# The front of a second transformer block, reordered: raw rows transposed, norms behind the matmuls, pool projection before the softmax transposes, a split router

## The chip, the core and the metric

One core of a Trainium2 chip runs the whole program in one launch. The metric is device time in microseconds (us) from start to end; lower is better. The engines named below are TensorE (PE; PEld is its weight load), VectorE (DVE), ScalarE (ACT), GpSimd (POOL) and SyncE (SP, which issues the weight loads). Each runs its own list of instructions in order and waits on semaphores.

## The reference, cut to what matters

Two blocks run one after the other on x of 256 tokens by 1024, all in float32. The first ends in a gated convolution FFN and a final RMS norm; its output is the second block's x:

```python
return rms_norm(h, norm_final_g)                  # end of the first block
# second block
h = rmsnorm(x, g_attn_norm)
u, q_lat, kv_lat, k_r = split(h @ w_in)           # 512, 256, 128, 32 columns
y_pool = pool_mixer(u, w_pool, b_pool, pool_scale)   # (window means - u) @ w_pool + b_pool, times pool_scale
y_attn = mla_attention(q_lat, kv_lat, k_r, ...)   # 8 heads: 64 plain + 32 rotated columns, causal softmax
mix = concat(rmsnorm(y_pool, g_out_pool), rmsnorm(y_attn, g_out_attn))
x = x + mix @ w_out
h = rmsnorm(x, g_ffn_norm)
x = x + moe(h, w_router, b_router, w_gate_up, ...)   # top 4 of 32 experts
return rmsnorm(x, g_final)
```

## The kernel before

The 256 tokens are two blocks of 128 rows (b = 0, 1); the 1024 columns are eight tiles of 128. `t.h` holds the residual rows, tokens on partitions. A matmul over the columns needs the rows transposed, which TensorE does against an identity, four 128x128 tiles into one bank of PSUM (eight banks), after which DVE or ACT copies the bank to SBUF.

Two lists written by hand, `RESULTS` and `RESULTS2`, fix the order in which the banks are filled and who drains each. A bank is opened when the result eight places earlier has been drained (`open_bank`); `filled` and `drained` turn a name into a semaphore and its value. For the second block the order is: `nT` (transposed normed rows), `lat0`, `lat1` (latents of q and kv and the raw rope columns), `u0`, `u1`, `qlT`, `kvT` (latents transposed), `qq`, `kv` (projections, drained by ACT), `qT`, `kT` (heads transposed), `s0` to `s7` (scores), `pm0`, `pm1` (pool matmul), `pss` (sums of squares of the pool output), `pt0` to `pt7` (softmax transposed), `av` (attention times values), `yt` (its transpose), `pa` and `pp` in turn (attention's and pool's half of the output projection, 512 columns for each of two row blocks), `rT` (rows transposed for the router), `lg` (logits), `rk` (ranks within an expert).

Norms: DVE and ACT make sums of squares, `finish_mean` the mean plus epsilon, POOL raises it to -0.5 (`rsqrt`, L434), DVE scales. Between the blocks there are two norms in a row: `end1` (with the gain in `t.g_rows`) and `attn`. Only after the second one are the rows transposed, and the gain `attn_norm` is multiplied in as the bank is copied (`turned`).

After `u1`, POOL makes the window sums and `t.diff`. The rope of q is done for each row block in six DVE operations (L1154 to L1156). ACT adds `b_pool`, DVE multiplies by `pool_scale`, squares, and multiplies by `g_out_pool`. The attention output is normed in rows, then transposed. `h` gets `pa` added and `pp` times the pool norm.

Mixture of experts: the router's logits give top-4, ranks and a list of jobs of up to 64 tokens of one expert. For each job TensorE gathers the normed rows into bank 6 (`gather`, a matmul with 0/1 matrix), they are copied to `t.x_T` (`copy_x`, ACT, L776), then come 64 matmuls with 8 chunks of gate and up weights of 1 MB, the activation, and 4 chunks of down weights. SP loads an expert's 12 chunks, each when the slot's last reader has finished. The first expert's chunks are asked for during the front, as results of the front free the ring of six slots; those of the next from the first job on. In a job, gather comes just before the transposed activation and the down projection.

Weights of the front go through the same ring (`front_chunks`, each with the result that reads it last). All vectors of gains are loaded as rows of two tables and transposed once at the start (`vec_T`).

Of the kernel before, what the change touches and what calls it, by code (L numbers as in the profile page):

```python
# [32 lines left out]
P = 128  # L33
T = 256
NB = T // P
D = 1024
# [27 lines left out]
VEC_A = dict(norm_mix=0, norm_ffn=8, attn_norm=16, ffn_norm=24, conv_w=32, conv_b=98)  # L64
VEC_B = dict(b_alpha=0, gla_g=2, b_pool=6, pool_scale=10, g_q_a=14, g_kv_a=16, g_out_pool=17, g_out_attn=21,
             b_gate=25)
ROWS_A, ROWS_B = 120, 41
# [19 lines left out]
    + [("lat0", "act"), ("lat1", "act"), ("u0", "act"), ("u1", "act")]  # L87
# [13 lines left out]
class Results:  # L101


    def __init__(self, order, s, banks):
        self.at = {name: n for n, (name, _) in enumerate(order)}
        self.order, self.s, self.banks = order, s, banks

    def bank(self, name):
        return self.banks[self.at[name] % 8]
# [42 lines left out]
def front_chunks(w):  # L152
# [19 lines left out]
    for n in range(2):  # L172
        second += [(cols(w["w_out_2"], 512 * n, 512, 4 * h), (4, 512), f"pp{n}1") for h in (1, 0)]
# [25 lines left out]
class Program:  # L199


    def __init__(self, nc, w, s, t, out, banks):
        self.nc, self.w, self.s, self.t, self.out, self.banks = nc, w, s, t, out, banks
        self.r1, self.r2 = Results(RESULTS, s, banks), Results(RESULTS2, Filled2(s), banks)
# [82 lines left out]
def sync_program(g, sp):  # L287
# [70 lines left out]
    for c, back in ((0, 6), (1, 5)):  # L358
        sp.wait_ge(*g.r2.filled(g.second[len(g.second) - back][2]))
        load_gu(0, c)  # L360
# [24 lines left out]
    for b in range(NB):  # L385
# [5 lines left out]
NORMS = (("mix", NB), ("gla", NB * GLA_H), ("ffn", NB), ("end1", NB), ("attn", NB), ("lat", 2 * NB), ("mla", NB),  # L391
         ("pool", NB), ("moe", NB), ("end2", NB))
WITH_ACT = ("ffn", "end1", "attn", "moe", "end2")
# [4 lines left out]
def gpsimd_program(g, pool):  # L398
# [37 lines left out]
    rsqrt("mix")  # L436
    pool.wait_ge(*g.r1.drained("att1"))
# [22 lines left out]
    rsqrt("attn")  # L460
# [35 lines left out]
    pool.tensor_tensor(t.diff[:], t.diff[:], t.u_pad[:, :, 16:], ALU.subtract).then_inc(s.diff_ready, 1)  # L496
    rsqrt("mla")
    rsqrt("pool")
# [6 lines left out]
def scalar_program(g, act):  # L505
# [32 lines left out]
    def square(name, sem, value):  # L538

        k = NORM_AT[name]  # L540
        act.wait_ge(sem, value)
        act.activation(t.x_n[:, 0, :], t.h[:, 0, :], ACT.Square, accum_out=t.msq[:, k, 0:1]).then_inc(s.act_msq, 1)
# [127 lines left out]
    square("end1", s.rows_ready, 1)  # L670


    square("attn", s.rows_ready, 2)
    act.wait_ge(s.msq_ready, NORM_AT["attn"] + 1)
    act.dma_start(t.g_rows[:], w["row_g_ffn_norm_2"].to_broadcast([P, D])).then_inc(s.late_in, 16)
    for b in range(NB):
        take(r2, f"lat{b}", t.lat[:, b, :], r2.bank(f"lat{b}")[:, 0:416])
    act.wait_ge(s.consts2, 1)
    for n in range(2):
        take(r2, f"u{n}", t.u_pad[:, 2 * n:2 * n + 2, 16:], pair(r2, f"u{n}"))  # L680
# [10 lines left out]
    for n in range(4):  # L691
        take(r2, f"qT{n}", t.q_T[0:QK, 2 * n:2 * n + 2, :], pair(r2, f"qT{n}")[0:QK])
# [8 lines left out]
    for h in range(MH):  # L701
        soft(h)
        if h == 3:
            for n in range(2):
                act.wait_ge(*r2.filled(f"pm{n}"))
                for i in range(2):
                    f = 2 * n + i
                    ins = act.activation(t.y_pool[:, f, :], pair(r2, f"pm{n}")[:, i, :], ACT.Identity,
# [1575 lines left out]
```

## Time and profile before

| | us |
|---|---|
| median of 3 runs (lowest, highest) | 1612.13 (1609.55, 1614.55) |
| the profiled execution's own time | 1612.03 |
| its span, first to last instruction | 1610.3 |
| granted TensorE clock, mean | 0.957 |
| first addition after the first block's FFN | 469.69 |
| first expert matmul | 633.01 |

| engine | busy us | share |
|---|---|---|
| PE | 1489.2 | 92% |
| PEld | 862.3 | 54% |
| DVE | 645.6 | 40% |
| ACT | 371.6 | 23% |
| POOL | 89.9 | 6% |

Busy is a share of the whole span; a stage has its own limit. The granted clock is a share of 2.4 GHz: 1.00 is that, 0.50 is 1.2 GHz. Times in rows count from the span's start.

### The profile page before, as it was taken

To read this page: it belongs to the slowest core of one execution; us is meant where nothing else is said; L and a number is where in the kernel's file an instruction comes from. 1 tells how busy PE (TensorE), PEld (TensorE's weight loads), DVE (VectorE), ACT (ScalarE), POOL (GpSimd) and SP (SyncE) were. 2 spreads that over 40 slices of the span, in tenths; PEclk is the share of its full clock that TensorE was granted. 3 is DMA by queue.
4 is the path that set the end of the run, shared out by engine and by line. 5 is a ranking of instruction groups with operands and counts; after the bars stand their busy time and mean duration, and the time that the engine had idled before them with its cause. 6 is when DMAs were issued, how large, how long until landed. Compare 5 with 4: busy or idle time off the path is not lost.

```text
span 1610.3 us, 21422 instructions
## 1 busy us (share of the span) xinstructions
PE 1489.2 (92%) x7752; PEld 862.3 (54%) x7753; DVE 645.6 (40%) x1099; ACT 371.6 (23%) x641; POOL 89.9 (6%) x117
## 2 busy tenths in 40 slices
PE   6999797999969687999999999999999999999995
PEld 5668574899956645444444444444444434434432
DVE  2134523766653423334333343333433333333233
ACT  0222102534411301222212222222222222122211
POOL 2000001232223000000000000000000000000000
PEclk9999897999989786999999999999999999999997
DMA  7332333555433512999999799999999999999993
GB/s 255 128 134 105 105 105 104 173 189 185 168 128 105 215 53 88 418 422 422 422 422 389 316 422 422 422 422 422 422 422 422 422 422 422 422 422 421 422 422 149
DMA packets 105179, 481.21 MB, mean 299 GB/s; under 512 B 10096, under 2 KB 34337, under 8 KB 56001
## 3 DMA queue, kind: packets, MB, share of 16 engines
q1 hardware_dynamic: 101408, 477.26, 73.6%
q10 hardware_dynamic: 3744, 3.59, 0.7%
q8 instruction: 18, 0.29, 0.1%
q14 instruction: 9, 0.07, 0.0%
HBM read 479.77 MB, written 1.05 MB: 299 GB/s over the span
## 4 chain that ended last, share of the span: by engine, by line
issue 63%; PE 32%; DVE 3%; POOL 1%; ACT 1%; DVEq 0%; POOLq 0%; ACTq 0%
PE bank L1455 8%; PE bank L1640 7%; PE bank L1463 6%; PE bank L1652 4%; PE bank L1609 2%; PE bank L1445 1%; PE bank L1752 1%; PE bank L1714 0%; POOL rstd L434 0%; PE bank L1742 0%; DVE u_lo L1106 0%; DVE h_lo L1065 0%; PE bank L1582 0%; PE bank L1587 0%; PE bank L1519 0%
## 5 line engine op out<-in xcount | busy, mean ns | idle before, releaser
L1824 PE MATMUL bank<-ring,x_T 128*64 128x512 f32 x1584 | 358.0, 597 | 21.8 <-DMA ring<-in_w_gate_up 21.7
L1824 PEld LDWEIGHTS bank<-ring,x_T 128*64 128x64 f32 x1584 | 116.6, 137 | 241.2 <-issue 241.2
L1893 PE MATMUL bank<-ring_b,act_T 128*64 128x512 f32 x1056 | 236.5, 601 | 0.5 <-ACT act_T L782 0.5
L1321 DVE TENSOR_TENSOR y_sum<-bank,y_cross 64x512 f32<-64x512 f32 x66 | 45.5, 689 | 312.6 <-ACT y_cross L740 311.6
L1352 DVE TENSOR_TENSOR h<-h,bank 128x512 f32<-128x512 f32 x128 | 82.3, 684 | 211.4 <-PE bank L1859 211.4
L1893 PEld LDWEIGHTS bank<-ring_b,act_T 128*64 128x64 f32 x1056 | 73.9, 138 | 146.2 <-issue 133.9
L1798 PEld LDWEIGHTS bank<-picks,x_n 128*128 128x128 f32 x1056 | 123.6, 196 | 26.3 <-issue 26.0
L1798 PE MATMUL bank<-picks,x_n 128*128 128x64 f32 x1056 | 128.2, 281 | 0.0
L1824 PE MATMUL bank<-ring_b,x_T 128*64 128x512 f32 x528 | 120.5, 598 | 0.0
L1455 PE MATMUL bank<-x_nT,ring 128*128 128x256 f32 x512 | 111.7, 380 | 0.8 <-DVE x_nT L865 0.8
L1455 PEld LDWEIGHTS bank<-x_nT,ring 128*128 128x128 f32 x512 | 96.9, 190 | 14.9 <-DVE x_nT L865 1.2
L1640 PE MATMUL bank<-h_hi,ff_hi 128*128 128x256 f32 x352 | 100.5, 285 | 1.9 <-DVE ff_lo L1080 1.9
L1640 PE MATMUL bank<-h_lo,ff_hi 128*128 128x256 f32 x352 | 100.2, 285 | 0.0
L1640 PE MATMUL bank<-h_hi,ff_lo 128*128 128x256 f32 x352 | 100.1, 284 | 0.0
L754 ACT ACTIVATE spread<-bank 128x256 fp32r<-128x256 f32 x33 | 12.6, 383 | 342.0 <-PE bank L1847 342.0
L764 ACT ACTIVATE cross<-bank 64x512 f32<-64x512 f32 x132 | 78.0, 591 | 49.8 <-PE bank L1824 49.8
L434 POOL TENSOR_TENSOR rstd<-msq,neg_half 128x2 f32<-128x2 f32 (+2 forms) x10 | 8.5, 856 | 1221.1 <-DVE msq L845 1177.8
L740 ACT ACTIVATE y_cross<-bank 64x512 f32<-64x512 f32 x33 | 19.6, 593 | 221.6 <-PE bank L1893 221.6
L1640 PEld LDWEIGHTS bank<-h_hi,ff_hi 128*128 128x128 f32 x352 | 68.2, 194 | 3.4 <-DVE ff_lo L1080 3.0
L1640 PEld LDWEIGHTS bank<-h_lo,ff_hi 128*128 128x128 f32 x352 | 68.2, 194 | 0.4
L1640 PEld LDWEIGHTS bank<-h_hi,ff_lo 128*128 128x128 f32 x352 | 68.1, 194 | 0.0
L1824 PEld LDWEIGHTS bank<-ring_b,x_T 128*64 128x64 f32 x528 | 36.8, 136 | 56.1 <-issue 55.6
(382 smaller groups left out, 1693.1 us busy)
## 6 DMA issues: line engine op xcount, KB each, us to landing
ring<-in_w_gate_up SPq DMA_DIRECT2D x192, 1024.0 KB, 22.1
ring_b<-in_w_down SPq DMA_DIRECT2D x128, 1024.0 KB, 21.2
ring_b<-in_w_gate_up SPq DMA_DIRECT2D x64, 1024.0 KB, 22.9
ring<-in_w_in SPq DMA_DIRECT2D x22, 1024.0 KB, 7.2
ring<-in_w_ffn_in SPq DMA_DIRECT2D x22, 1024.0 KB, 5.1
ring<-in_w_ffn_out SPq DMA_DIRECT2D x11, 1024.0 KB, 4.8
ring<-in_w_out SPq DMA_DIRECT2D x8, 1024.0 KB, 5.1
ring<-in_w_branch_sb SPq DMA_DIRECT2D x2, 1024.0 KB, 5.0
```

The lines of the kernel that those rows point to most:

```text
L740: act.activation(t.y_cross[0:SLOTS, :], g.banks[4][SLOTS:, :], ACT.Copy).then_inc(s.y_crossed, 1)
L764: act.activation(t.cross[here, n // 2, :], g.banks[n][there, :], ACT.Copy).then_inc(s.crossed, 1)
L1321: dve.tensor_tensor(t.y_sum[rows, :], g.banks[4 + c][rows, :], t.y_cross[rows, :], ALU.add).then_inc(s.y_summed, 1)
L1352: dve.tensor_tensor(t.h[:, b, cols], t.h[:, b, cols], g.banks[4 + c][:], ALU.add).then_inc(s.added, 1)
L1455: ins = pe.matmul(bank[:, j * T:(j + 1) * T], wk[:, f * P:(f + 1) * P], src[:, k, :], start=(k == 0), stop=(k == len(weights) - 1))
L1463: ins = pe.matmul(bank[:, 0:n], src[:, k, b * P:(b + 1) * P], wk[:, c0:c0 + n], start=(k == 0), stop=(k == len(weights) - 1))
L1609: ins = pe.matmul(bank[:, q * T:(q + 1) * T], chunk(g, n + q, (4, 512))[:, k, cols], src[:, k, :], start=(k == 0), stop=(k == 3))
L1640: ins = pe.matmul(bank[:, f * T:(f + 1) * T], wt[:, k, f * P:(f + 1) * P], ht[:, k, :], start=(k == 0 and part == 0), stop=(k == KT - 1 an ...
L1652: ins = pe.matmul(banks[2 * b + c][:], ut[:, q, k, b * P:(b + 1) * P], wt[:, k, 512 * c:512 * c + 512], start=False, stop=last, skip_group ...
L1798: ins = pe.matmul(banks[6][:, f * SLOTS:(f + 1) * SLOTS], t.h_n[:, b, f * P:(f + 1) * P], t.picks[:, b, :], start=(b == 0), stop=(b == 1))
L1824: ins = pe.matmul(banks[n][rows, :], t.x_T[:, c, :], job_slot(g, c)[:, 512 * n:512 * n + 512], start=False, stop=(pair == PAIRS - 1), skip ...
L1893: ins = pe.matmul(banks[4 + n][rows, :], t.act_T[:, k, SLOTS * (c // 2):SLOTS * (c // 2) + SLOTS], job_slot(g, GU + c)[:, D * i + 512 * n: ...
```

## The change

Nothing in the mathematics changes, but where factors are applied does:

- `nT` transposes the raw rows `t.h` as soon as each 128x512 quarter is added. The gain multiplied in on the way out is `gain2` = final gain times attention gain. The factor of a token, both norms in one, is applied behind the matmuls: as ACT's scale for `lat`, and for `u` by a row of token factors spread over all partitions with a diagonal and a matmul with ones (`rb`). POOL works out this factor from the sums of squares of h and of h times the gain. The normed `h` itself is made later by ACT.
- The rope of q is six operations on both row blocks. K is transposed first. `pm` goes before the scores, `pss` and `pp` between scores and softmax transposes. ACT makes the pool output and its square straight from the bank, with products of the vectors that POOL makes at the program's start.
- The attention output is transposed without its norm; `pa` is scaled by it when it is added.
- The router works on raw rows: `rT` and its matmuls are split by column half, the gain is in `w_router`, the norm is applied to the logits. ACT makes the normed rows for the gather without the gain; the gain comes in when DVE, no longer ACT, copies the gathered rows (`take_x`), in every job.
- The first expert's chunks 2 to 5 are asked for in the order 3, 5, 2, 4, behind the results that now free their slots.

```diff
 RESULTS2 = (
     [(f"nT{b}{h}", "dve") for b in range(2) for h in range(2)]
-    + [("lat0", "act"), ("lat1", "act"), ("u0", "act"), ("u1", "act")]
+    + [("lat0", "act"), ("lat1", "act"), ("rb", "dve"), ("u0", "dve"), ("u1", "dve")]
     + [("qlT", "dve"), ("kvT", "dve")]
...
-    + [(f"qT{n}", "act") for n in range(4)] + [(f"kT{n}", "dve") for n in range(4)]
-    + [(f"s{h}", "dve") for h in range(MH)]
-    + [("pm0", "act"), ("pm1", "act"), ("pss", "dve")]
+    + [(f"kT{n}", "act") for n in range(4)] + [(f"qT{n}", "dve") for n in range(4)]
+    + [("pm0", "act"), ("pm1", "act")] + [(f"s{h}", "dve") for h in range(MH)] + [("pss", "dve")]
+    + [(f"pp{n}{b}", "dve") for n in range(2) for b in range(2)]
     + [(f"pt{h}", "act") for h in range(MH)] + [("av0", "dve"), ("av1", "dve")]
-    + [("yt0", "dve"), ("yt1", "dve")]
-    + [(f"{s}{n}{b}", "dve") for n in range(2) for b in range(2) for s in ("pa", "pp")]
-    + [(f"rT{b}{h}", "act") for b in range(2) for h in range(2)] + [("lg", "dve"), ("rk", "dve"), ("gT", "act")]
+    + [("yt0", "dve"), ("yt1", "dve"), ("pa00", "dve"), ("pa01", "dve"), ("pa10", "dve")]
+    + [("rT00", "act"), ("rT10", "act"), ("pa11", "dve"), ("rT01", "act"), ("rT11", "act")]
+    + [("lg0", "dve"), ("lg1", "dve"), ("rk", "dve"), ("gT", "act")]
 )
```

SP and POOL:

```diff
-    for c in (2, 3, 4, 5):
-        sp.wait_ge(*g.r2.filled(g.second[len(g.second) - RING + c][2]))
+    for c, user in ((3, "pp01"), (5, "pp11"), (2, "pa01"), (4, "pa11")):
+        sp.wait_ge(*g.r2.filled(user))
         load_gu(0, c)
...
     rsqrt("end1")
-    rsqrt("attn")
+    pool.wait_ge(s.rstd_ready, NORM_AT["end1"] + 1)
+    k, k1 = NORM_AT["attn"], NORM_AT["end1"]
+    mean, r1 = t.rstd[:, k, 0:NB], t.rstd[:, k1, 0:NB]
+    step(pool.tensor_tensor(mean, r1, r1, ALU.mult))
+    step(pool.tensor_tensor(mean, mean, t.msq[:, k1, NB:2 * NB], ALU.mult))
+    step(pool.tensor_scalar(mean, mean, EPS, None, ALU.add))
+    step(pool.tensor_tensor(mean, mean, t.neg_half[:, 0:NB], ALU.pow))
+    pool.tensor_tensor(mean, mean, r1, ALU.mult).then_inc(s.rstd_ready, 1)
```

DVE:

```diff
+    for b, n in ((0, 0), (0, 1), (1, 0)):
+        add_rows(b, n)
+    for h in range(2):
+        turned_rows(0, h)
+    add_rows(1, 1)
+    for h in range(2):
+        turned_rows(1, h)
...
+    for b in range(NB):
+        dve.tensor_tensor(t.x_n[:, b, :], t.h[:, b, :], t.g_rows[:], ALU.mult).then_inc(s.h_gained, 1)
...
+        dve.tensor_scalar(t.diag[:, b, :], t.ident[:], rstd("attn", b), None, ALU.mult).then_inc(s.diag_ready, 1)
+    bank, done = out_of(r2, "rb")
+    dve.tensor_copy(t.token_scale[:], bank[:, 0:T]).then_inc(done, 1)
...
+    for n in range(2):
+        bank, done = two(r2, f"u{n}")
+        dve.tensor_tensor(t.u_pad[:, 2 * n:2 * n + 2, 16:], bank,
+                          t.token_scale[:].unsqueeze(1).to_broadcast([P, 2, T]), ALU.mult).then_inc(done, 1)
...
-    for b in range(NB):
-        dve.tensor_scalar(t.y_attn[:, b, :], t.y_att[:, b, :], rstd("mla", b), None,
-                          ALU.mult).then_inc(s.y_attn_ready, 1)
...
+    def take_x(m, o):
+
+        dve.wait_ge(s.gathered, nth(m, o, 1, 1))
+        dve.tensor_tensor(t.x_T[:], g.banks[6][:].rearrange("p (k n) -> p k n", k=KT),
+                          spread(vec(t, "ffn_norm", 0, KT), SLOTS), ALU.mult).then_inc(s.x_ready, 1)
+
+    take_x(None, 0)
     dve.wait_ge(s.top_exp, 1)
...
         swiglu(m, 1)
+        if not final:
+            take_x(m, 2)
```

ACT:

```diff
+    act.wait_ge(s.rstd_ready, NORM_AT["attn"] + 1)
+    for b in range(NB):
+        take(r2, f"lat{b}", t.lat[:, b, :], r2.bank(f"lat{b}")[:, 0:416],
+             scale=t.rstd[:, NORM_AT["attn"], b:b + 1])
...
+    for n in range(2):
+        act.wait_ge(*r2.filled(f"pm{n}"))
+        for i in range(2):
+            f = 2 * n + i
+            act.activation(t.y_pool[:, f, :], pair(r2, f"pm{n}")[:, i, :], ACT.Identity, bias=t.pool_b2[:, f:f + 1],
+                           scale=t.pool_g2[:, f:f + 1]).then_inc(s.pool_y, 1)
...
+    act.wait_ge(s.rstd_ready, NORM_AT["moe"] + 1)
+    for b in range(NB):
+        act.activation(t.h_n[:, b, :], t.h[:, b, :], ACT.Copy,
+                       scale=t.rstd[:, NORM_AT["moe"], b:b + 1]).then_inc(s.h_ready, 1)
```

TensorE:

```diff
-    pe.wait_ge(s.x_n_ready, 3 * NB)
-    turn(r2, "nT", t.x_n)
-    pe.wait_ge(*r2.drained("nT11"))
+    for b in range(NB):
+        for h in range(2):
+            pe.wait_ge(s.rows_added, 2 * b + h + 1)
+            turn_quarter("nT", t.h, b, h)
...
+    pe.wait_ge(s.diag_ready, NB)
+    bank = open_bank(r2, "rb")
+    for b in range(NB):
+        ins = pe.matmul(bank[:, b * P:(b + 1) * P], t.ones[:], t.diag[:, b, :], start=True, stop=True)
+    ins.then_inc(s.filled2, 1)
...
+    pe.wait_ge(s.pool_y, 4)
+    for c in range(2):
+        for b in range(NB):
+            project_out("pp", t.y_pool, c, b)
...
+    for c, b in ((0, 0), (0, 1), (1, 0), (1, 1)):
+        project_out("pa", t.ya_T, c, b)
+        if (c, b) == (1, 0):
+            for b2 in range(NB):
+                pe.wait_ge(*r2.drained(f"pa0{b2}"))
+                turn_quarter("rT", t.h, b2, 0)
...
+    for b in range(NB):
+        router(b, 0)
+    for b in range(NB):
+        pe.wait_ge(*r2.drained(f"pa1{b}"))
+        turn_quarter("rT", t.h, b, 1)
+    for b in range(NB):
+        router(b, 1).then_inc(s.filled2, 1)
```

## Rows read from the trace of the kernel before

**Rows 1.** Windows: busy time of each engine, granted clock, DMA share and GB/s.
```profile
core 0: us, PE busy (x) PEld busy (x) DVE busy (x) ACT busy (x) POOL busy (x), PEclk, DMA share, GB/s
534.00:535.40 1.40, 0.48 (x5) 0.22 (x3) 1.28 (x2) 0.00 (x0) 0.00 (x0) 1.00 0.00 0
603.30:633.00 29.70, 20.28 (x103) 18.16 (x102) 14.07 (x40) 6.28 (x10) 0.70 (x1) 0.59 0.31 111
885.00:895.00 10.00, 10.00 (x50) 3.31 (x46) 2.75 (x8) 1.90 (x3) 0.00 (x0) 1.00 0.00 0
1175.00:1575.00 400.00, 380.42 (x2006) 171.59 (x2008) 142.51 (x282) 85.63 (x173) 0.00 (x0) 1.00 1.01 422
```

**Rows 2.** SP's queue in order of time: start, us, issues of an expert's first chunks.
```profile
894.22 8.51 SPq L353 DMA_DIRECT2D ring<-in_w_gate_up  x6
...
1175.09 11.11 SPq L353 DMA_DIRECT2D ring<-in_w_gate_up  x6
...
1532.47 11.61 SPq L353 DMA_DIRECT2D ring<-in_w_gate_up  x6
```

**Rows 3.** The chain that ended last, 469 to 567 us: start, us, what.
```profile
469.69 0.70 DVE h L1121
...
486.01 13.14 PE bank L1463 x32
499.16 13.81 PE bank L1455 x64
...
514.24 5.41 PE bank L1463 x16
...
527.89 6.59 PE bank L1714 x32
...
552.63 5.24 PE bank L1742 x24
...
558.43 8.06 PE bank L1752 x48
```

**Rows 4.** Order in time, 520 to 583 us: rope, sums of squares, first output projections.
```profile
523.43 2.39 DVE L1156 TENSOR_TENSOR q_tok<-rope_tmp 128x128 f32<-128x128 f32 x1
...
549.05 3.58 PE L1735 MATMUL bank<-ones,y_sq 128*128 128x1 f32 x16 [6.38 <-DVE y_sq L1195]
...
573.01 6.28 PE L1463 MATMUL bank<-ring,ya_T 128*128 128x512 f32 x8 [0.78 <-DVE ya_T L1218]
...
579.12 3.60 PE L1463 MATMUL bank<-ring,y_pool 128*128 128x512 f32 x8
```

**Rows 5.** Order in time, 603 to 638 us: router, gather, first expert.
```profile
603.42 0.75 DVE L1228 SCALAR_TENSOR_TENSOR h<-bank,rstd,h 128x512 f32<-128x512 f32 x1 [2.82 <-PE bank L1463]
...
606.46 2.48 DVE L1235 SCALAR_TENSOR_TENSOR x_n<-h,rstd,g_rows 128x1024 f32<-128x1024 f32 x2 [0.81 <-POOL rstd L434]
...
608.99 3.59 PE L1445 MATMUL bank<-ident,x_n 128*128 128x128 f32 x16 [5.68 <-DVE x_n L1235]
...
613.27 4.79 PE L1776 MATMUL bank<-w_router,h_T 128*128 128x32 f32 x32 [0.69 <-ACT h_T L536]
...
618.09 0.22 DVE L1242 TENSOR_TENSOR logits<-bank,b_router 128x64 f32<-128x64 f32 x1 [8.76 <-PE bank L1776]
...
623.35 7.09 PE L1798 MATMUL bank<-picks,x_n 128*128 128x64 f32 x32
...
627.30 0.59 DVE L1295 TENSOR_REDUCE gate_e<-one_hot 128x64 f32<-128x256 f32 x1
...
633.01 5.25 PE L1824 MATMUL bank<-ring,x_T 128*64 128x512 f32 x16
```

**Rows 6.** Order in time, 653 to 670 us: a job's activation, x_T copy, next job.
```profile
653.88 0.69 DVE L1377 SCALAR_TENSOR_TENSOR act<-up,gate 128x512 f32<-128x512 f32 x1
...
655.96 0.60 ACT L776 ACTIVATE x_T<-bank 128x512 f32<-128x512 f32 x1
...
662.93 7.07 PE L1824 MATMUL bank<-ring,x_T 128*64 128x512 f32 x32
```

More of the change, by code:

```diff
@@ L691, in scalar_program @@
     for n in range(4):
-        take(r2, f"qT{n}", t.q_T[0:QK, 2 * n:2 * n + 2, :], pair(r2, f"qT{n}")[0:QK])
+        take(r2, f"kT{n}", t.k_T[0:QK, 2 * n:2 * n + 2, :], pair(r2, f"kT{n}")[0:QK])
+    act.wait_ge(s.gains, 4)
+    for n in range(2):
[5 more added lines that the diff above has]
+    for n in range(2):
+        for i in range(2):
+            f = 2 * n + i
+            ins = act.activation(t.y_sq[:, f, :], pair(r2, f"pm{n}")[:, i, :], ACT.Square, bias=t.pool_b1[:, f:f + 1],
+                                 scale=vec(t, "pool_scale", f))
+            if i == 0:
+                step(ins)
+        ins.then_inc(r2.drained(f"pm{n}")[0], 1)
     def soft(h):
@@ L771, in sigmoid @@
         act.activation(t.sig[:], t.gate[:], ACT.Sigmoid, scale=SWIGLU_ALPHA).then_inc(s.sig_ready, 1)
-    def copy_x(m, o):
-        act.wait_ge(s.gathered, nth(m, o, 1, 1))
-        act.activation(t.x_T[:], g.banks[6][:].rearrange("p (k n) -> p k n", k=KT), ACT.Copy).then_inc(s.x_ready, 1)
     def turned_act(m, o):
@@ L800, in turn @@
         turned_act(m, 1)
-        if not final:
-            copy_x(m, 2)
     act.wait_ge(s.jobs_ready, 1)
@@ L1134, in vector_program, with add_rows, turned_rows @@
-    mean_squares_with_act("attn")
+    def add_rows(b, n):
+        cols = slice(512 * n, 512 * n + 512)
+        dve.tensor_tensor(t.h[:, b, cols], t.h[:, b, cols], g.banks[2 * b + n][:], ALU.add).then_inc(s.rows_added, 1)
+    def turned_rows(b, h):
+        bank, done = out_of(r2, f"nT{b}{h}")
+        dve.tensor_tensor(t.h_nT2[:, 4 * h:4 * h + 4, b * P:(b + 1) * P], bank[:].rearrange("p (k n) -> p k n", k=4),
+                          spread(t.gain2[:, 4 * h:4 * h + 4], P), ALU.mult).then_inc(done, 1)
@@ L1191, in vector_program, with add_out @@
             dve.tensor_scalar(t.row_m[:, hs, :], t.row_m[:, hs, :], -1.0, None, ALU.mult).then_inc(s.row_max, 1)
-    dve.wait_ge(*r2.drained("pm1"))
-    step(dve.tensor_tensor(t.y_pool[:], t.y_pool[:], spread(vec(t, "pool_scale", 0, 4), T), ALU.mult))
-    dve.tensor_tensor(t.y_sq[:], t.y_pool[:], t.y_pool[:], ALU.mult).then_inc(s.pool_sq, 1)
-    dve.wait_ge(s.pool_sq, 1)
-    dve.tensor_tensor(t.y_pool[:], t.y_pool[:], spread(vec(t, "g_out_pool", 0, 4), T), ALU.mult).then_inc(s.pool_y, 1)
+    bank, done = out_of(r2, "pss")
+    k = NORM_AT["pool"]
+    dve.tensor_scalar(t.msq[:, k, 0:NB], bank[:, 0:NB], 1.0 / 512, EPS, ALU.mult, ALU.add).then_inc(done, 1)
+    dve.wait_ge(*r2.drained("pss"))
+    dve.sem_inc(s.msq_ready, 1)
+    dve.wait_ge(s.h_scaled, NB)
+    have_rstd("pool")
+    def add_out(name, norm, n, b):
+        cols = slice(512 * n, 512 * n + 512)
+        bank, done = out_of(r2, f"{name}{n}{b}")
+        dve.scalar_tensor_tensor(out=t.h[:, b, cols], in0=bank[:], scalar=rstd(norm, b), in1=t.h[:, b, cols],
+                                 op0=ALU.mult, op1=ALU.add).then_inc(done, 1)
+    for n in range(2):
+        for b in range(NB):
+            add_out("pp", "pool", n, b)
     dve.wait_ge(s.prob_ready, NB * MH)
     step(dve.reciprocal(t.row_l[:], t.row_l[:]))
-    bank, done = out_of(r2, "pss")
-    dve.tensor_copy(t.pool_sum[:], bank[:, 0:NB]).then_inc(done, 1)
-    dve.wait_ge(*r2.drained("pss"))
     for b in range(NB):
@@ L1730, in tensor_program @@
         ins.then_inc(s.filled2, 1)
-    pe.wait_ge(s.pool_sq, 1)
+    pe.wait_ge(*r2.drained("kT3"))
+    pe.wait_ge(*r2.drained("qT3"))
+    for h in range(MH):
+        bank = open_bank(r2, f"s{h}")
+        pe.matmul(bank[:, 0:P], t.q_T[0:QK, h, 0:P], t.k_T[0:QK, h, 0:P], start=True, stop=True)
+        pe.matmul(bank[:, P:3 * P], t.q_T[0:QK, h, P:], t.k_T[0:QK, h, :], start=True, stop=True).then_inc(s.filled2, 1)
+    pe.wait_ge(*r2.drained("pm1"))
     bank = open_bank(r2, "pss")
@@ L1975, in __init__ @@
         self.small_in = new("small_in")
-        self.late_in = new("late_in")
+        self.gains = new("gains")
+        self.rows_added = new("rows_added")
+        self.h_gained = new("h_gained")
+        self.h_scaled = new("h_scaled")
+        self.diag_ready = new("diag_ready")
+        self.k_roped = new("k_roped")
         self.end_in = new("end_in")
```

234 lines of the change are left out of this document (113 added, 121 removed).

## Prediction

> **What bounds the kernel now.** I read the waits first, then the stages by time, then SP's queue, and last the chain of waits and the order in time from the end of the first block's FFN (469.7 us) to the first expert matmul (633.0). From 894 on the time is a stream of expert weights. SP's issue of an expert's first chunks comes at 894.22 and at 1175.09, ten experts later: 28.1 us each, TensorE's pace; from there to 1532.47 it is twelve in 357.4 us, 29.8 each, the DMA's pace [rows 2]. In that last stretch TensorE works 380 of 400 us and the DMA engines all of it; but from 885 to 895, at a job that loads nothing, the DMA queue stands still [rows 1]. So the DMA bound is no fixed end. The queue has already run empty once and starts again when TensorE frees a buffer, and TensorE's jobs are paced back to their first one at 633.0. Whatever moves 633.0 moves 894.22, the DMA stretch and the end by the same amount, unless a job itself changes. The question is therefore how much later or earlier the first expert matmul starts, and whether the loop stays as long.
>
> The front before it takes 163.3 us. The reader should see in the chain that it is serial: additions from 469.69, latent projection 486.01, u projection 499.16, q and kv projections 514.24, head transposes 527.89, softmax transposes 552.63, attention times values 558.43 [rows 3]. At 573.01 the output projections start [rows 4] and end at about 603.4; router, top-k, gather and first job preparation follow to 633.01 [rows 5].
>
> **Front, first part (469.7 to the end of the u projection, U).** Old: TensorE stands still for norm, gain, norm, scaling until transposes and gains are done at 486.0. New: raw rows are transposed as they are added. DVE does three additions (469.69 + 3 x 0.70 = 471.8), two gains while TensorE has transposed the first row block (0.70 each, 473.2), the fourth addition (473.95). TensorE's program turns the fourth quarter before the projection, so it waits for this addition, turns it in 0.5 to 0.9 (a sixteenth of 3.59 each at the low clock [rows 5], half at the high one) and starts at about 474.8 instead of 486.01: 11.2 less. I give the projection its old 13.15 to 499.16 [rows 3], low-clock start included (32 matmuls of 416 columns at the full rate, worked out from 3.60 for 8 of 512 [rows 4], would be 11.7, so up to 1.5 less). It ends at 487.9. Off the path: two gain products and two squares on DVE, 1.24 each [rows 5], then POOL's five small operations, taken at 3 us together, and the two diagonals, ready at about 484.6; they have 3 us of cover, and beyond that cost one for one. New on the path: the two matmuls that spread the norm over columns, 0.5. Then the u projection, 13.8 as before. U = 487.9 + 0.5 + 14.0 = 502.4 against 513.0: **10.6 less**, bounds 9 to 13. POOL's constants now come later (11.5 us of them) and hold the latent norm back to about 496.6; the u matmuls run until 502.4, so this is covered with 4 us to spare.
>
> **From U to the first expert matmul: old 120.0 (513.0 to 633.0).** New, step by step after U:
> - u's copy moves from ACT to DVE ahead of the q gain: old q matmuls at U + 1.3, new + 1.6. q and kv 8.8, last copy 0.95: 11.3. This is a loss of 0.3.
> - K is turned first and needs no rope of q. The rope, 12 operations (old 520.3 to 527.8, among them 2.39 beside a POOL operation against 0.3 undisturbed [rows 4]), becomes 6 operations of twice the size, 2.6 us undisturbed and about 5.5 beside POOL, done by U + 13.5, behind K's transposes. The old stall of 4.8 us in front of 527.89 goes. 32 transposes: 6.6 at the old, mostly low clock [rows 3], 3.5 at the high one; I take 5.6. At 16.9.
> - pool matmuls, moved in front of the scores, 1.9: 18.8. Scores 5.3: 24.1. Sums of squares: old 3.58 [rows 4], at the high clock 1.9; I take 2.9: 27.0. Their inputs now come from eight ACT operations (0.46 each, 3.7), done by about U + 21.8 under the scores; banks of the last scores come free then, a microsecond before they are wanted.
> - pool projection: half of the 64 matmuls, 4 x 3.43 = 13.7: 40.8. It covers the whole softmax: row maxima at U + 24.5 and 28.6, 7.0 us of exponentials done at U + 32.2. The time is not new work; it leaves the later block.
> - softmax transposes and copies: old 552.63 to 558.43, 5.8 [rows 3]; ACT's eight copies of 0.5 bound it from below at 4.5; I take 5.2: 46.0. Values 8.06 [rows 3], at the high clock about 6; 7.2: 53.2.
> - norm of attention behind the matmul: old 566.5 to 573.01 is 6.5; new is one product, a quarter's transposes, one gain: 2.6 (55.8). The squares and POOL's power run beside the first projection.
> - attention projection 4 x 3.43 = 13.7, two router quarters turned in it 1.3, low-clock start 2.5 (old 6.28 - 3.60 = 2.7 [rows 4]; bounds 0 and 2.9): 73.3. Old end of the projections was U + 90.35.
> - router: old, the last addition at 603.42 is followed by the norm (3.0 us to 606.46), scaling 2.48, 16 transposes 3.59, copies, 32 router matmuls 4.79, and the logits at 618.09, which is 14.8 after the last projection's end [rows 5]. New, half of the router runs on the first half of the rows; after the projection come 16 matmuls (2.0 to 3.5), eight transposes (1 to 1.8), the last copy and 8 matmuls: logits at + 5.5 to + 7.1, 6.3 taken. Norm (+ 3.1) and ACT's scaled rows (+ 6.5) are ready before the gather. Gain 8.5.
> - from logits to the first expert matmul, old 14.9. One part gets longer: the expert input's copy moves to DVE in front of the gates. DVE waits there for the gather (7.09 [rows 5]), and only then copies 0.7 and makes the gates, 1.65 (five operations, of which the last takes 0.59 from 627.30 on [rows 5]). Queued behind them on TensorE are the turned gates, the bias and the first expert matmul: 1.7 later than old. New total after the projection 6.3 + 14.7 + 1.6 = 22.6.
>
> Sum: 73.3 + 22.6 = 95.9 against 120.0, **24.1 less**. With the first part 34.7 less.
>
> **The loop.** Each job's copy of the gathered rows (0.60 on ACT, 655.96) becomes a DVE product of 0.7 after the activation product, which starts at 653.88 and takes 0.69; it ends at about 655.6. The next job's matmuls read it at 662.93 [rows 6]: 7 us of cover, the down projection. Price 0. At the start, one more small load and POOL's gain products are hidden (0.7 us of slack before the first scaling; POOL has nothing else until the attention mask).
>
> **Total.** The profiled execution took 1612.0 (span 1610.3, 1.7 around it), 0.1 below the median of 1612.1. 1612.0 - 34.7 = 1577.3; 1577.
>
> **The clock, weighed.** From 527.89 to 534.48 TensorE did transposes alone, 6.59 us for 32, 0.21 each and so mostly at the low level of 1.2 GHz; yet from 534.0 the granted clock is 1.00, 2.4 GHz [rows 1, 3]: the high level came back under them. By the Trainium skill, "TensorE: Matmul & The Clock Gate", Part 4 (PE-mode transpose), transposes do not count as work that releases the clock. This trace disagrees; by that rule the time would be that of the first rival.
>
> **Rivals.**
> - Clock low in the middle: K's and Q's transposes let it fall to 1.2 GHz before pool matmuls and scores. Those double: 0.9 + 1.9 + 5.3 + 0.7 and a low-clock start of the pool projection 2.8, 11.6 in all: 1589. For it: the router's and gather's thin matmuls in the stretch 603.3 to 633 show 0.59 [rows 1], and the gather took 0.22 per matmul. Against it: the rise at 534.
> - Clock higher than before, since gaps vanish: 1.5 at the latents, 2.5 at the attention projection, 3.5 in the gather: 7.5 less, 1570.
> - DMA hides it: the end would stay at a fixed date, 1612, if the weight stream were the bound from the start. The idle queue at 885 to 895 speaks against it [rows 1].
> - Slower: the DVE product of the loop is late. If it ran only behind the next y sums, some 3.5 us after the down projection, 17 jobs at TensorE's pace would each pay 3.5 and 15 at the DMA's pace 1.8 (29.8 - 28.1 is slack): 87 more, 1664. It decides from 1.9 us per job (17 x 1.9 + 15 x 0.2 = 35). Against it: the program places it 7 us ahead of its reader.
>
> **How the numbers follow.** The main case 0.74 (1571 to 1584), low clock 0.11, high clock 0.10, DMA hides it 0.02, slower 0.02, and 0.01 for waits not seen here that cost more than the gain. The range 1568 to 1590 takes in the first three but their tails. 0.3% is 4.8 us, about what a measurement of this kernel can tell from no change. Faster 0.95, same 0.02, slower 0.03.
>
> **What the changed profile would show.** Latent projection starting near 475; u ending near 502; q turned after k with no stall over 1 us between; pool projection between scores and softmax transposes, at the full clock; attention projection starting near 558 and ending near 576; logits 6 us later; first expert matmul near 598; then the same 28.1 and 29.8 us. What would make me wrong: a low clock in the scores, a stall at the spread matmul or at the pool squares, or a job of the loop longer than 28.1.

## The result and the profile after

The changed kernel took 1566.68 us (1565.0 to 1569.74) against 1612.49 (1609.55 to 1614.55) for the kernel before, a ratio of 0.9719, 95% interval 0.9697 to 0.9741: 45.8 us less. The forecast was 1577.3, so it is faster, as forecast, but the time is 10.6 below the forecast and 1.3 below the range. The profiled execution took 1567.46, with a span of 1565.7 and a mean granted clock of 0.976 (0.957 before).

The chain that ended last, from the FFN's additions to the last quarter of the attention projection: start, us, what. It answers to [rows 3].

```profile
471.34 1.88 DVE h L1135 x3
...
475.08 0.66 PE bank L1721 x4
475.73 11.18 PE bank L1508 x32
486.91 0.45 PE bank L1738 x4
487.35 13.82 PE bank L1500 x64
501.17 0.44 PE bank L1747 x4
...
512.39 2.47 DVE q_tok L1216
514.91 1.95 PE bank L1773 x16
516.86 1.73 PE bank L1787 x8
...
523.83 1.68 PE bank L1800 x16
525.51 13.84 PE bank L1508 x32
...
539.72 3.18 ACT prob_T L551 x8
542.94 5.58 PE bank L1829 x48
...
550.74 10.57 PE bank L1508 x24
561.30 0.88 PE bank L1721 x8
562.18 3.45 PE bank L1508 x8
```

The windows of the same stretch, to be held against the 0.59 of 603.3 to 633 and the low durations in [rows 3, 4]:

```profile
core 0: us, PE busy (x) PEld busy (x) DVE busy (x) ACT busy (x) POOL busy (x), PEclk, DMA share, GB/s
475.00:503.00 28.00, 27.15 (x112) 20.01 (x113) 14.62 (x45) 4.44 (x6) 12.00 (x51) 1.00 0.22 69
503.00:515.00 12.00, 10.45 (x41) 5.97 (x40) 7.45 (x8) 7.03 (x16) 10.75 (x12) 1.00 0.90 324
...
540.00:550.00 10.00, 8.64 (x75) 7.93 (x72) 2.29 (x6) 2.89 (x8) 0.00 (x0) 1.00 0.74 310
550.00:566.00 16.00, 15.27 (x46) 7.56 (x46) 4.76 (x10) 2.12 (x4) 0.69 (x1) 1.00 0.18 67
566.00:586.00 20.00, 15.19 (x90) 13.60 (x89) 11.71 (x39) 6.45 (x9) 0.69 (x1) 0.69 0.23 86
```

The column to read is PEclk: TensorE has the 2.4 GHz level from the FFN to the end of the attention projection, without a break. TensorE never stands still for long there: the chain passes from one of its stages to the next with waits under 1.2 us. The router, which had it only in part before, has it whole: its 32 matmuls take 1.87 and 1.97 where they took 4.79. The clock falls at 573.9, behind TensorE's wait of 2.8 for the top-k, and the gather and the first expert's matmuls have the low level (0.50 from 574 to 590). The order in time there is (answering to [rows 5]):

```profile
565.45 1.87 PE L1851 MATMUL bank<-w_router,prob_T 128*128 128x32 f32 x16
...
570.48 0.25 DVE L1276 SCALAR_TENSOR_TENSOR logits<-bank,rstd,b_router 128x32 f32<-128x32 f32 x1 [0.57 <-PE bank L1851]
...
575.38 7.06 PE L1881 MATMUL bank<-picks,x_n 128*128 128x64 f32 x32
...
582.48 0.69 DVE L1328 TENSOR_TENSOR x_T<-bank,vec_T 128x512 f32<-128x512 f32 x1 [4.34 <-PE bank L1881]
...
586.53 5.77 PE L1907 MATMUL bank<-ring,x_T 128*64 128x512 f32 x16
```

Behind the first expert matmul the loop keeps its pace. SP's issues of an expert's first chunks answer to [rows 2]; the first gap is ten experts at 28.09, the second twelve at 29.8, and the DMA queue is again all but empty at the job that loads nothing (DMA share 0.09 from 840 to 850):

```profile
848.36 8.51 SPq L353 DMA_DIRECT2D ring<-in_w_gate_up  x6
1129.27 11.09 SPq L353 DMA_DIRECT2D ring<-in_w_gate_up  x6
1486.66 11.64 SPq L353 DMA_DIRECT2D ring<-in_w_gate_up  x6
```

The first expert matmul came 46.5 earlier (586.53 against 633.01), the issue at 894.22 came 45.9 earlier, the one at 1532.47 45.8 earlier, and the end 44.6 earlier. So what the front gained reached the end but for 1.9, as the argument on the empty queue said.

### The profile page after: what moved, and what is told of

Same layout as the page of the kernel before. It is cut to its first block, busy times and chain, and to the rows that moved or that the text cites. A ratio compares the mean times of both kernels' runs of the same rounds, so it can differ in the third digit from the quotient of the medians.

```text
span 1565.7 us, 21446 instructions
## 1 busy us (share of the span) xinstructions
PE 1473.2 (94%) x7756; PEld 847.5 (54%) x7757; DVE 660.6 (42%) x1122; ACT 359.6 (23%) x614; POOL 92.3 (6%) x126
## 4 chain that ended last, share of the span: by engine, by line
issue 64%; PE 31%; DVE 3%; POOL 1%; ACT 1%; DVEq 0%; POOLq 0%; ACTq 0%
PE bank L1500 8%; PE bank L1685 7%; PE bank L1508 6%; PE bank L1697 4%; PE bank L1654 2%; PE bank L1490 0%; PE bank L1829 0%; DVE u_lo L1122 0%; DVE h_lo L1081 0%; PE bank L1627 0%; PE bank L1632 0%; POOL rstd L434 0%; PE bank L1564 0%; PE bank L1553 0%; PE bank L1795 0%
```

## The experiments

All are edits of the changed kernel except the fifth. Unless another is named, each is held against 1566.68. The profile of each is its own, so a stage is compared by its length and by its distance from the FFN's first addition (F) or the end of the u projection (U), not by its date: F itself lay between 468.3 and 472.1 in kernels that are the same up to it.

**1. Transposes behind the norms.** TensorE's `nT` waits for the factor of both norms; everything else stays behind the matmuls.

```diff
-    for b, n in ((0, 0), (0, 1), (1, 0)):
-        add_rows(b, n)
...
+    for b in range(NB):
+        for n in range(2):
+            add_rows(b, n)
...
+    pe.wait_ge(s.rstd_ready, NORM_AT["attn"] + 1)
     for b in range(NB):
         for h in range(2):
             pe.wait_ge(s.rows_added, 2 * b + h + 1)
```

> The changed kernel with its first step undone in time: the rows are transposed only after both norms' factor is known (TensorE waits for POOL's last small operation; DVE does all additions, the gain products and squares first). The wait alone, counted from the changed kernel's own rows: transposes start at 482.4 instead of 472.1, latent projection at about 486.8 instead of 475.7, 11 us more. Theory A (what my forecast lacked is the clock: TensorE no longer idles long enough between the FFN and the router for it to fall): the 11 us of idling also bring the 1.2 GHz level back, transposes 1.5 and latent projection 2.0 longer, so 14 us more than the changed kernel, 1581, with windows at 0.50 between 476 and 489. Rival B (the clock plays no part there, all of it is shorter waits): 11 us more, 1578, latent projection 11.2 long.

Measured: 1576.22 (1574.85 to 1586.26), 9.5 more. Windows of the wait, the transposes and the latent projection:

```profile
470.00:480.20 10.20, 0.00 (x1) 0.01 (x1) 7.21 (x12) 2.30 (x4) 2.30 (x7) 0.68 0.16 51
480.20:483.90 3.70, 3.70 (x17) 3.70 (x18) 2.07 (x3) 0.00 (x0) 2.77 (x14) 0.51 0.00 0
483.90:495.10 11.20, 11.20 (x34) 6.11 (x34) 1.08 (x3) 0.61 (x1) 5.01 (x30) 1.00 0.00 0
```

The clock fell in the wait, and the 16 transposes ran at the low level; but when the projection began it was back, and its 11.2 are those of the changed kernel. By the chain the projection starts 14.2 after F in place of 4.4, 9.8 later, and the total is up by 9.5. From the first transpose to the projection it is 3.5, against 2.1 in experiment 2, where the clock stayed up: so about 1.3 of the 9.8 is the low clock under the transposes and 8.5 the order. No low-clock start of the projection came on top. Carrying one over from before would have been wrong here too.

**2. The same with idle matmuls in the wait.** 20 matmuls of 512 columns whose product nobody reads.

```diff
+    landed(g.n_second)
+    pe.wait_ge(s.rows_added, 1)
+    for _ in range(20):
+        pe.matmul(banks[7][:], t.ident[:], t.ring[:, g.n_second % RING, 0:512], start=True, stop=True)
     pe.wait_ge(s.rstd_ready, NORM_AT["attn"] + 1)
```

> The same as e1_norms_first, but TensorE does 20 matmuls of 512 columns whose result nobody reads while it waits (8.6 us of its 10 us of waiting). Theory A: the clock stays at 1.00, the latent projection takes 11.2 us, and the kernel is 3 us faster than e1_norms_first, 1578. Rival B: no difference to e1_norms_first.

Measured: 1581.95 (1578.36 to 1584.33). The count was wrong: one such product is two instructions and 0.87 us. The twenty ran from 469.44 to 486.85, and the transposes began 18.1 after F in place of 10.6, 7.5 beyond the wait. So it doesn't test the price of the wait; what it shows is the transposes at a granted clock of 1.00, 1.91 in place of 3.68. A version with 8:

> The changed kernel with its transposes held back behind both norms, as in the second experiment, but with 8 idle 512-column matmuls (0.87 us each as measured there, 7.0 us in all) in place of 20, so that they fill the wait of 9.2 us and do not overrun it. The idle products are never read. Without them the transposes took 3.68 at the low clock and the version ran 1576.2. If waits cost only their own length and the clock costs what the low rate adds, this runs 1.8 less in the transposes (4 x 0.45) and nothing else: 1574.4, and the changed kernel plus 9.2 less 1.0 hidden is 1575. If the clock's state at the end of the wait were worth more (a start at the low clock of the latent projection and what follows), the gap to 1576.2 would be 4 or more: 1572.

Measured: 1575.57 (1574.34 to 1577.35). The idle matmuls ended at 476.6, TensorE then stood for 2.60, and the transposes were low again (window 479.2 to 482.6: 0.54; 3.47 us). The 1.8 expected there did not come, since the clock fell in the last 2.60 (at 1.00 to 478.5, lower before 479.2); the difference of 0.6 to experiment 1 is inside the spreads.

**3. The pool projection back behind the attention's transposes.**

```diff
-    + [(f"pp{n}{b}", "dve") for n in range(2) for b in range(2)]
     + [(f"pt{h}", "act") for h in range(MH)] + [("av0", "dve"), ("av1", "dve")]
-    + [("yt0", "dve"), ("yt1", "dve"), ("pa00", "dve"), ("pa01", "dve"), ("pa10", "dve")]
+    + [("yt0", "dve"), ("yt1", "dve")] + [(f"pp{n}{b}", "dve") for n in range(2) for b in range(2)]
+    + [("pa00", "dve"), ("pa01", "dve"), ("pa10", "dve")]
```

> The changed kernel with the pool projection put back behind the transposed attention output, in front of the attention projection. Waits alone: softmax transposes can start at 525.5 but are paced by ACT's exponentials, which end at 531.6 in the changed kernel; values start at 532.6 instead of 542.9 - 13.8 = 529.1: 3.5 us more, 1570. Theory A adds the clock: sparse work for 7 us, values 2 us longer and 2.7 for a low-clock start of the pool projection: 8 us more, 1575. If the move was worth nothing: 1567.

Measured: 1578.43 (1578.09 to 1580.41), 11.7 more, beyond both. The chain of waits:

```profile
525.73 3.62 ACT score L732 x16
529.34 3.02 ACT prob_T L551 x8
...
532.40 10.50 PE bank L1825 x48
542.90 1.91 PE bank L1831 x8
...
545.59 27.23 PE bank L1508 x56
```

U is at 498.84. Values start at U + 33.6; in the changed kernel they start at U + 41.8, of which 13.8 are the pool projection, so 5.6 of softmax now lie open: the chain runs through ACT's exponentials and copies. Values take 10.50 where they took 5.58, and the 56 projection matmuls 27.23 + 0.87 + 3.45 for the rest where 28.7 were needed, 2.8 more. So of 13.8 between U and the end of the projections, 5.6 is the wait and some 7.7 is the clock behind it. The granted clock is 0.50 from 525 to 550: it fell while ACT's exponentials held the softmax transposes back, and stayed low through values that TensorE did without a break.

**4. The router whole, behind the norm.** All four quarters are transposed after ACT's scaled rows.

```diff
-        if (c, b) == (1, 0):
-            for b2 in range(NB):
-                pe.wait_ge(*r2.drained(f"pa0{b2}"))
-                turn_quarter("rT", t.h, b2, 0)
+    pe.wait_ge(s.h_ready, NB)
+    for h in range(2):
+        for b in range(NB):
+            turn_quarter("rT", t.h, b, h)
```

> The changed kernel with the router put back behind the norm: all four row quarters are transposed only after ACT has made the scaled rows, then all router matmuls; the factor is still applied to the logits. Changed kernel: last output projection ends 565.6, logits 4.8 later. Here norm 3.0, ACT's two scalings 2.3, transposes 3.6, copy 0.7, router matmuls 4.8 at the low clock: logits 14.5 after the projection, which itself ends 0.9 earlier: 9 us more, 1576. If only the column split mattered and not the norm, under 1 us.

Measured: 1572.55 (1571.29 to 1579.28), 5.9 more. TensorE stands 5.30 before the transposes, which then take 3.67 at the low clock; the router itself took 3.95 in one piece. The profiled execution was the slowest, and shows why the spread is wide: its values took 8.01 and not 5.58, though nothing before them differs. The clock fell at about 545, in the middle of the values, and the attention projection behind them took 2.8 longer.

```profile
542.46 8.01 PE L1829 MATMUL bank<-v_tok,prob_T 128*128 128x64 f32 x48 [0.97 <-ACT prob_T L551]
...
575.29 3.67 PE L1721 MATMUL bank<-ident,h 128*128 128x128 f32 x16 [5.30 <-ACT x_n L742]
```

**5. The kernel before, with idle matmuls in three of its waits** (12 before the transposes, 6 before the sums of squares, 3 before the attention's transposes). Nothing is moved.

```diff
+    landed(g.n_second)
+    idle_matmuls(banks[7], t.ring[:, g.n_second % RING, 0:512], 12)
...
+    idle_matmuls(bank, t.x_n[:, 0, 0:512], 6)
+    pe.wait_ge(s.pool_sq, 1)
...
+        if b == 0:
+            idle_matmuls(bank, t.x_n[:, 0, 0:512], 3)
+        pe.wait_ge(s.y_attn_ready, b + 1)
```

> The kernel before with nothing moved; TensorE only does matmuls that nobody reads (512 columns of float32, 0.87 us each at 2.4 GHz) where it stood idle: 12 after the FFN while the norms are made (11.9 us of idling), 6 before the pool's sums of squares (6.4), 3 after the attention values (3.7). Theory A: the clock stays at 1.00 from 469 to about 575, and the work that the change also has runs at its speed there: transposes 1.8 less, latent projection 2.0, sums of squares 1.7, softmax transposes and copies 2.2, values 2.4, first output projection 2.7, some 10 us in all minus an overrun of up to 2: 1603. That would be the clock's share of the 46 us. Rival B: 1612 or slower.

Measured: 1605.18 (1601.95 to 1608.33) against 1612.13 (1605.34 to 1617.41), ratio 0.9957, interval 0.994 to 0.9974: 7.0 less, from work that nobody reads.

```profile
471.69 10.46 PE L1674 MATMUL bank<-ring,ident 128*128 128x512 f32 x24
483.75 1.97 PE L1445 MATMUL bank<-ident,x_n 128*128 128x128 f32 x16 [1.60 <-DVE x_n L1137]
486.99 11.44 PE L1463 MATMUL bank<-ring,h_nT 128*128 128x416 f32 x32 [1.27 <-DVE h_nT L865]
...
527.15 3.65 PE L1721 MATMUL bank<-ident,q_tok 128*96 128x128 f32 x16 [4.81 <-DVEq L1177]
...
555.14 5.57 PE L1760 MATMUL bank<-v_tok,prob_T 128*128 128x64 f32 x48 [0.74 <-ACT prob_T L536]
```

Latent projection 11.4 (13.14 in [rows 3]), values 5.6 (8.06). At the end of the projections this profile is 9.6 ahead of the one before, counted from F; at the first expert matmul it is 7.2 ahead, because its router matmuls met the low clock whole (7.03 in place of 4.79). So where the clock is low later on had moved too. The head transposes, in front of which the stall of 4.8 was left as it was, are still slow (3.65 for the first 16).

**6. Q's heads turned before K's**, as before; the rest stays.

```diff
-    + [(f"kT{n}", "act") for n in range(4)] + [(f"qT{n}", "dve") for n in range(4)]
+    + [(f"qT{n}", "dve") for n in range(4)] + [(f"kT{n}", "act") for n in range(4)]
...
-    turn_heads("kT", [t.k_tok[:, b] for b in range(NB)])
     pe.wait_ge(s.q_roped, 1)
     turn_heads("qT", [t.q_tok[:, b, :].rearrange("p (h x) -> p h x", h=MH) for b in range(NB)])
+    turn_heads("kT", [t.k_tok[:, b] for b in range(NB)])
```

> The changed kernel with Q's heads turned before K's, as in the kernel before; all else stays. Q's rope ends 13.7 after the end of the u projection, K's transposes could start 11.2 after it. TensorE then stands still for 3.5 before the transposes in place of 0.94 and 0.62. Theory A (only the wait counts): the first score comes 2.0 later, 1568.7. Theory B (the clock falls in the stall, as it did in the kernel before): the 32 transposes take 5.6 to 7.5 in place of 3.9 and perhaps the pool matmuls double, so 3.7 to 6.5 later in all, 1570.4 to 1573.

Run beside the changed kernel again:

> The changed kernel unchanged, to have its spread beside the other two of this call. It took 1566.68 (1565.0 to 1569.74). Both theories: 1566 to 1568, with single runs from 1562 to 1572, since the granted clock changes level at other places in other runs (values took 5.58 in one profile and 8.01 in two).

Measured: 1569.87 (1567.0 to 1575.33), and 1567.22 (1566.04 to 1572.38) for the changed kernel, 2.65 more; the spreads overlap. The trace is plainer. Order in time of the version with Q first:

```profile
512.03 2.60 PE L1773 MATMUL bank<-ident,q_tok 128*96 128x128 f32 x16 [3.67 <-DVE q_tok L1216]
514.42 2.94 PE L1773 MATMUL bank<-ident,k_tok 128*96 128x128 f32 x16
517.20 1.89 PE L1787 MATMUL bank<-diff,ring 128*128 128x256 f32 x8
```

After a stall of 3.67 the transposes take 5.5 together in place of 3.9 (granted clock 0.72 from 513 to 519). It is back at about 516.5, under the last of the transposes, and so for the pool matmuls. The first score comes at U + 21.0 in place of U + 17.4: 3.6, of which 2.0 is the wait and 1.6 the clock.

**7. The first job's copy behind the gates** on VectorE.

```diff
-    take_x(None, 0)
     dve.wait_ge(s.top_exp, 1)
...
+    take_x(None, 0)
```

> The changed kernel with the first job's copy of the gathered rows put behind the gates on DVE instead of in front of them. In the changed kernel's trace the gates end at 584.7 because DVE waited for the gather until 582.5; 1.65 us of gates come before the gather's end here, so TensorE's transposed gates start at 583.2 instead of 584.9 and the first expert matmul at 584.9 instead of 586.5: 1.6 us less, 1565. If the loop's start were set by something else (the expert's chunks): no change, 1566.7.

Measured: 1568.9 (1561.95 to 1572.12), no gain to be seen. From the end of the projections to the first expert matmul its profile has 19.85 against 20.9, so about 1 is there. In that profile the values took 8.01 and the attention projection behind them 2.8 longer, as in experiment 4, which covers it; the median of six runs shows no gain either.

**8. Idle matmuls before the ranks**, on top of 7, to hold the clock up for the gather.

```diff
+    pe.wait_ge(s.end_in, 16)
+    for _ in range(3):
+        pe.matmul(banks[0][:], t.ident[:], t.g_rows[:, 0:512], start=True, stop=True)
```

> The changed kernel with the first job's copy of the gathered rows behind the gates on VectorE, and three idle 512-column matmuls (0.87 us each, 2.6 in all, never read) between the router's logits and the ranks, where TensorE stands still for the top-k. In the changed kernel the granted clock falls at 573.9 and the gather of 32 thin matmuls takes 7.06. Theory A (the clock falls because TensorE pauses there, and the gather is slow for the clock alone): the gather takes 3.6 to 5, the first expert matmul comes 3 earlier than without the idle matmuls, 1.6 more from the copy: 1562. Rival B (thin matmuls of 64 columns let the clock fall or cost 0.22 each at any clock): gather stays near 7, 1565 at most.

Measured: 1561.09 (1557.92 to 1568.59), ratio 0.9709, interval 0.9684 to 0.9734. Order in time:

```profile
567.66 2.82 PE L1864 MATMUL bank<-g_rows,ident 128*128 128x512 f32 x6
...
572.62 3.76 PE L1884 MATMUL bank<-picks,x_n 128*128 128x64 f32 x32 [0.15 <-DVE picks L1304]
```

The gather takes 3.76 where it took 7.06, with a granted clock of 1.00 from 566 to 586. Its price is the clock's, not that of thin matmuls. The changed kernel's own loop says the same: there a gather of the same shape runs at the high level.

```profile
605.08 3.79 PE L1881 MATMUL bank<-picks,x_n 128*128 128x64 f32 x32
```

F to the first expert matmul is 109.4 against 115.2, 5.8 less, of which about 1 is experiment 7's.

**9. The last job's bias matmuls behind its down projection.** They stood in front of it, at 6.63 in the profile after, while the activation was being made.

```diff
-        if final:
-            down_bias(m, 1)
-        else:
+        if not final:
...
+        if final:
+            down_bias(m, 1)
```

> The changed kernel with the last job's bias matmuls put behind its down projection. At the end of the changed kernel TensorE does these 8 matmuls (6.63 us, at the low clock) in front of the transposed activation, which was ready at 1534.3 and is turned at 1538.9; behind the down projection there are 3.8 us of idling for them (1548.9 to 1552.7). 4.6 us less if they run at 2.4 GHz there (3.7 us), 1562; 1.7 less if the low clock meets them there (6.6 us).

Measured: 1564.98 (1561.42 to 1569.27), ratio 0.971, interval 0.9687 to 0.9733: 1.7 less in the median, inside the spread. In its profile the bias matmuls take 3.70 behind the down projection, and the stretch from the last gate and up matmul to the last y sums is 3.9 shorter; but the last chunk was waited for by 1.48 and its matmuls took 5.35 in place of 3.65, so that from F to the end only 0.4 is left. Whether the edit is to blame for that wait is not settled.

**10. 7, 8 and 9 together**, run twice.

> The changed kernel with three edits together: the first job's copy behind the gates (1.6 by the stretch), three idle matmuls before the ranks (3 if theory A of the gather holds, 0 by its rival), and the last job's bias matmuls behind its down projection (1565.0 against 1566.7 alone, 1.7). Theory A: 1566.7 - 1.6 - 3 - 1.7 = 1560.4. Rival B: 1563.4.

> The version with the first job's copy behind the gates, three idle matmuls before the ranks and the last job's bias matmuls behind its down projection, again, now beside the changed kernel. It took 1559.84. If its gain is its own: 1560, 6 to 7 under the changed kernel of this call. If the changed kernel merely had slower runs on its chip: within 3 of it.

Measured: 1559.84 (1557.28 to 1560.38), ratio 0.968, interval 0.9662 to 0.9697; and 1560.69 (1554.1 to 1565.05), ratio 0.9686, interval 0.9663 to 0.9709, where the changed kernel beside it had 1567.22, ratio 0.9741, interval 0.9726 to 0.9757. The two intervals do not meet. So this version beats both kernels, the changed one by 6.5. The gather took 5.31 and 5.84 in its two profiles: the clock now falls within it, and not before it, though TensorE had stood for less than 0.5 at a time since the idle matmuls.

**11. The loop's copy behind the next y sums**, the forecast's slower rival made real.

```diff
     swiglu(m, 1)
-        if not final:
-            take_x(m, 2)
...
+        take_x(m, 1)
```

> The changed kernel with the loop's copy of the gathered rows on DVE behind the next y sums, the placement that my slower rival named. The copy then ends some 3.2 us after the down projection instead of 7 us before its reader. All 32 jobs would take 28.1 + 3.2 = 31.3 us, above the DMA's 29.8, so the loop is paced by TensorE throughout: 17 x 3.2 + 15 x 1.5 = 77 us more, 1644. If the down projection's wait did not matter: 1567.

Measured: 1667.85 in a single run, 101 more. Order in time around a job's start:

```profile
650.49 0.69 DVE L1328 TENSOR_TENSOR x_T<-bank,vec_T 128x512 f32<-128x512 f32 x1
...
651.42 7.09 PE L1905 MATMUL bank<-ring,x_T 128*64 128x512 f32 x32 [3.12 <-DVE x_T L1328]
...
972.59 7.09 PE L1905 MATMUL bank<-ring,x_T 128*64 128x512 f32 x32 [3.13 <-DVE x_T L1328]
...
1004.02 8.78 PE L1905 MATMUL bank<-ring,x_T 128*64 128x512 f32 x32 [3.13 <-DVE x_T L1328]
```

In the changed kernel the same product runs where its reader is 7.4 away:

```profile
607.93 0.69 DVE L1419 SCALAR_TENSOR_TENSOR act<-up,gate 128x512 f32<-128x512 f32 x1
608.91 0.69 DVE L1328 TENSOR_TENSOR x_T<-bank,vec_T 128x512 f32<-128x512 f32 x1 [0.29 <-PE bank L1881]
...
616.98 3.60 PE L1907 MATMUL bank<-ring,x_T 128*64 128x512 f32 x15
```

The mechanism of that rival is as stated, and does not happen in the changed kernel. Its price was set somewhat low: 22 jobs took 706.8 (SP's issues at 880.42 and 1587.24) against 638.3. They take 32.1 each throughout (the tenth issue after 880.42 comes at 1201.56), which is 4.0 more in the first ten, where 3.5 had been allowed, and 2.4 more in the last twelve, where 1.8 had. The wait is 3.1 in every job; in some the clock falls behind it (0.66 granted from 1005 to 1010), and the first 32 matmuls take 8.78 in place of 7.09. So the same wait costs its own length in one job and 1.7 more in the next.

## Why the prediction was right in kind and wrong in size

The forecast was right that the date of the first expert matmul decides, on the order of the chain, on the covers and on the loop's price of 0. The waits vanished as worked out. What failed is the step that took the low clock of the kernel before over into stages whose wait had been removed: the latent projection at its old 13.15, transposes, sums of squares and values between their two durations, and a low-clock start of 2.5 in the attention projection. In its place the granted clock was 1.00 in all of them, and they took 9.4 less. Term by term, forecast and measured:

| | forecast | measured |
|---|---|---|
| F to the latent projection | 5.1 | 4.4 |
| latent projection ("its old 13.15, low-clock start included") | 13.15 | 11.18 |
| spread norm, u projection | 14.5 | 14.3 |
| U to K's transposes | 11.3 | 11.2 |
| head transposes ("I take 5.6") | 5.6 | 4.5 with a wait of 0.6 |
| pool matmuls and scores | 7.2 | 7.0 |
| sums of squares ("I take 2.9") | 2.9 | 1.68 |
| pool projection | 13.7 | 13.84 |
| softmax transposes and copies ("ACT's eight copies of 0.5") | 5.2 | 3.6 |
| values ("7.2") | 7.2 | 5.58 |
| to the attention projection | 2.6 | 2.2 |
| attention projection ("low-clock start 2.5") | 17.5 | 14.9 |
| projections' end to the first expert matmul | 22.6 | 20.9 |

From F on the front is 13.4 shorter than forecast. The clock's terms are latent projection 2.0, transposes 1.7 (3.9 busy), sums of squares 1.2, values 1.6, attention projection 2.5 and 0.4: 9.4. ACT's copies took 0.40 each and not 0.5, 1.6 with what hung on them. The remaining 2.4 are small terms, mostly the logits, at + 4.9 where 6.3 was taken out of + 5.5 to + 7.1; the low end of that was for the high clock, which the router had, so 0.8 of this too is the clock's. Given back were 1.65, since the FFN ended later in the profiled execution (the code up to there is the same), and 1.9 behind the first expert matmul, of which the last job's bias matmuls are 2.9 (6.63 against 3.69) and the first job's 0.5, less a faster down projection: 13.4 - 3.6 = 9.8, the miss (1577.3 against 1567.5 in the profiled execution).

That the 9.4 are the clock's is shown from two sides: experiment 5 takes 7.0 out of the kernel before with its order untouched, and experiments 3 and 6 put a wait back and get the clock's price behind it, 7.7 on a wait of 5.6 and 1.6 on one of 2.0. Experiment 1 shows that it need not reach the next long stage: TensorE stood for 10.6, the transposes were slow, and the projection behind them was not.

Two slips in the forecast's arithmetic change little. The u projection is given as 13.8 and summed as 14.0, and the stretch from the logits on is given as 14.9 and 1.7 longer but summed as 14.7 + 1.6, so that the sum is 0.3 short there.

The rival "clock higher" (1570) had the mechanism and two of its three places: 1.5 at the latents came as 2.0, 2.5 at the attention projection came. Its 3.5 in the gather did not (7.06), with TensorE still standing 2.8 for the top-k before it; experiment 8 shows what it takes. It left out transposes, sums of squares and values, and it had a chance of 0.10 only. That its 1570 lies nearer to the result than 1577 is so in part because the missing 3.5 and the places left out nearly cancel. The rival "clock low in the middle" falls: the clock stayed at 1.00 through all 32 transposes. The rule weighed there, that transposes do not release the clock (the Trainium skill, "TensorE: Matmul & The Clock Gate", Part 4), finds no support in these runs: in experiment 6 the clock fell and came back again within the 32 transposes, 0.50 from 514 to 516 and 0.74 from 516 to 517, as it had come back under them in the kernel before (1.00 from 534.0, the transposes ending at 534.48). "DMA hides it" falls with the 45.8 that reached the last issue.

What each part is worth can be read from its undoing: norms behind the matmuls 9.5, pool projection before the softmax 11.7, split router 5.9, K first 2.65. Together that is 29.8 of 45.8; the norm of the attention behind its matmul (6.5 to 2.2 by the trace) was not undone by itself, and the parts share the clock, so they need not add up. Where in a given run the clock changes level is not settled: values took 5.58 in most profiles of the changed order and 8.01 in two, behind identical work.

## What to carry to other kernels

When a change takes a wait of TensorE away, read the price of the stages behind it from rows at 1.00 in the granted clock, not from their old rows; keep the old duration as the upper bound, since the clock can still fall in a given run (experiments 4 and 7). In a stretch that TensorE paces, the long independent matmuls belong into the waits of the thin ones, and where there is no such work, idle matmuls can pay (6.5 here with two small moves, 7.0 in the kernel before), provided their own duration is measured and fits the wait. A copy moved to another engine costs by its place in that engine's list: here nothing when it is done 7.4 ahead of its reader, and 101 (one run) when it stands behind the sums.

## What had not been expected of the hardware

- One float32 matmul of 512 columns in the program is two instructions of 0.43 us (17.41 for twenty, 40 instructions, at a granted clock of 1.00), twice what I had counted for the idle ones.
- Single runs of the kernel before lay between 1605.3 and 1617.4, and of the changed one between 1565.0 and 1572.4. Both spreads are wider than the 4.8 us that the forecast took as the smallest difference to be told.
- A wait of 3.1 us in every job of experiment 11 was followed by 32 matmuls in 7.09 or in 8.78.
- A gather of 32 matmuls of 64 columns took 3.76, 5.31, 5.84 or 7.06: all of it at a granted clock of 1.00 in the first, part of it in the next two, and all at 0.50 in the last.
